# A two-block transformer kernel on one core: six buffers for the u rows in place of four, six places in the weight ring in place of eight

## What is computed

```
def peer(h, w_query, sub_keys, u, v):
    # 8 heads, product keys (2 x 128 sub-keys), top-16 per half -> 256 candidates -> top-16
    ...
        best_s, best_pos = lax.top_k(cand_s, PEER_TOPK)
        expert = jnp.take_along_axis(cand_i, best_pos, axis=-1)
        gate = jax.nn.softmax(best_s, axis=-1)
        u_sel = jnp.take(u, expert, axis=0)
        v_sel = jnp.take(v, expert, axis=0)
        act = jax.nn.gelu(jnp.einsum('btd,bthkd->bthk', hx, u_sel, ...))
        return jnp.einsum('bthk,bthkd->btd', (gate * act).astype(h.dtype), v_sel)
```

## Time and profile before

| | |
|---|---|
| time, median of 3 runs (lowest to highest) | 2198.12 us (2190.49 to 2200.41) |
| span of the profiled execution | 2300.7 us |
| mean granted TensorE clock in it | 0.924 |
| busy: TensorE / weight loads / VectorE / ScalarE / GpSimd | 1853.9 / 1098.1 / 1383.9 / 710.3 / 1045.5 us |
| moved by DMA | 708.03 MB, of it 553.72 MB by the gathers (queue q0) and 150.65 MB by SP's queue (q1) |

### The profile page before, as it was taken

How to read it: one execution, slowest core, us unless ns; L and a number is a source line. 1 busy time by engine, 2 the same in 40 slices (tenths; PEclk the granted TensorE clock), 3 DMA queues, 4 the chain that set the end, 5 groups by cost and what they waited for, 6 DMA issues and landing times. The chain is left out here.

```text
span 2300.7 us, 22295 instructions
## 1 busy us (share of the span) xinstructions
PE 1853.9 (81%) x7068; PEld 1098.1 (48%) x7075; DVE 1383.9 (60%) x3053; ACT 710.3 (31%) x1634; POOL 1045.5 (45%) x1067
## 2 busy tenths in 40 slices
PE   8798766767977787687878866988676898888998
PEld 6554222212643462245445522533232696667996
DVE  2566767645367547755775586555455446456874
ACT  2233433321154113313331233011001344444653
POOL 0365666675447556754666566666666000000000
PEclk7899999997988899988889998999999899998999
DMA  5799999998999999999889999999999354344563
GB/s 185 256 386 376 351 366 350 346 358 308 409 335 352 380 409 368 347 365 387 292 317 402 409 354 350 371 406 381 372 367 370 120 174 123 115 137 133 188 179 116
DMA packets 194851, 708.03 MB, mean 308 GB/s; under 512 B 21784, under 2 KB 23072, under 8 KB 194480
## 3 DMA queue, kind: packets, MB, share of 16 engines
q0 software_dynamic: 152064, 553.72, 63.7%
q1 hardware_dynamic: 40960, 150.65, 19.0%
q10 hardware_dynamic: 1712, 2.24, 0.3%
HBM read 704.81 MB, written 1.06 MB: 307 GB/s over the span
## 5 line engine op out<-in xcount | busy, mean ns | idle before, releaser
L577 PE MATMUL ps<-a,diag 128*128 128x512 f32 (+1 forms) x1872 | 952.9, 647 | 283.7 <-DMA a<-in_peer_v,eidx 114.0
L1738 DVE SCALAR_TENSOR_TENSOR a<-a,ps 128x1024 f32<-128x1024 f32 x512 | 621.4, 1215 | 287.2 <-DMA a<-in_peer_u,eidx 227.4
L406 POOL DMA_INDIRECT a<-in_peer_u,eidx x528 | 527.0, 998 | 494.7 <-DVE a L1738 257.2
L577 PEld LDWEIGHTS ps<-a,diag 128*128 128x128 f32 (+1 forms) x1872 | 351.6, 201 | 825.8 <-issue 678.4
L416 POOL DMA_INDIRECT a<-in_peer_v,eidx x528 | 517.1, 979 | 244.3 <-issue 143.5
L850 PE MATMUL ps<-a_r 128*128 128x256 f32 (+1 forms) x1648 | 392.8, 330 | 19.9 <-DVE a_r L1917 7.3
L1131 ACT ACTIVATE gel<-dots 128x1 f32<-128x1 f32 x528 | 102.6, 201 | 836.9 <-DVE a L1738 482.1
L850 PEld LDWEIGHTS ps<-a_r 128*128 128x128 f32 x1648 | 279.1, 191 | 52.2 <-DVE a_r L1917 8.1
L1911 DVE TENSOR_TENSOR ring_r<-wring,a_r 128x1024 fp32r<-128x1024 f32 x142 | 173.3, 1222 | 138.7 <-ACT a_r L1369 138.6
L1369 ACT ACTIVATE a_r<-wring 128x1024 fp32r<-128x1024 f32 x142 | 149.5, 1054 | 81.8 <-PE ps L850 81.7
L850 PE MATMUL ps<-a_r,ring_r 128*128 128x256 f32 x512 | 144.7, 283 | 0.0
(11 more groups left out here) (263 smaller groups left out, 1583.9 us busy)
## 6 DMA issues: line engine op xcount, KB each, us to landing
wring<-in_units SPq DMA_DIRECT2D x268, 512.0 KB
a<-in_peer_u,eidx POOLq DMA_INDIRECT x528
a<-in_peer_v,eidx POOLq DMA_INDIRECT x528
cs2c<-in_cs SPq DMA_DIRECT2D x1, 1792.0 KB
a<-in_poolm SPq DMA_DIRECT2D x1, 1632.0 KB, 8.9
h<-in_xin SPq DMA_DIRECT2D x2, 512.0 KB, 4.2
bcF<-in_bc_rows SPq DMA_DIRECT2D x2, 512.0 KB, 13.4
cs2c<-in_units SPq DMA_DIRECT2D x2, 512.0 KB, 14.5
```

The costliest lines, as they stand in the source:

```text
L406: g.indirect_dma_start(ug[:, n % NU, :], None, peer_u, bass.IndirectOffsetOnAxis(ap=eidx[:, t, k:k + 1], axis=0))\
L577: last = nc.tensor.matmul(ps[0:P, 6 + j, :], diag[:, pe_slots[n] % 4, 0:P], vg[:, k % NV, j * 512:(j + 1) * 512], start=False, stop=False)
L1738: v.scalar_tensor_tensor(ug[:, n % NU, :], ug[:, n % NU, :], 1.0, hnm if t == 2 else ps2(4), ALU.mult, ALU.mult, accum_out=dots[:, k % 8:k ...
```

## The change

```
-R = 8
-NU = 4
+R = 6
+NU = 6
 NV = 8
...
-                if n == SPLIT0:
+                if n == U0["mem_k"]:
 
                     sp.wait_ge(S("eidx"), tk_number(1, 1))
                     sp.dma_start(memx[:, :, :], mem.rearrange("(t p) d -> p t d", p=128)).then_inc(S("ld_mem"), 16)
                     sp.dma_start(bcL, bc_rows[4:5, :].to_broadcast([128, D])).then_inc(S("ld_g"), 16)
```

## The result

| | median of 4 runs | lowest to highest |
|---|---|---|
| before | 2197.6 us | 2190.49 to 2200.41 |
| after | 2167.69 us | 2166.09 to 2169.31 |

The ratio is 0.9863, 95% interval 0.9848 to 0.9877: 30 us or 1.4% faster. The forecast was 2146, 52 us less than before. Direction and range held, but only 30 of the 52 us came.

The account below looks back on a forecast made before the run. No engine is busy throughout; gathers stall on too few u buffers, leaving DMA under its 409 GB/s ceiling. Parts of 54 + 0 + 0 us off a 2300.7 us span scale 2198.12 to 2146 us, forecast 2110 to 2172, range 2105 to 2187.

Parts of the forecast that it names:

- Part 1: Gather part: two more u buffers shorten GpSimd's waits for dots; 54 us won, between 20 and 88.
- 64 us over 25 stalls: Gather part, stall by stall: smallest of GpSimd's wait, VectorE's wait after it and 5.1 us; five reach the cap.
- The ceiling that the prediction took: Gather stages: the most that deeper buffers can give, summed by stage to 88 us.
- its own example: GpSimd stall at 340.04 to 345.89 us, 4.91 us idle while VectorE is in the top-k; six buffers would remove it.
- the smaller of room and u waits: Each gather stage: gain is the smaller of DMA room below 409 GB/s and VectorE's u waits, or GpSimd's dot waits if less.
- rival (a): VectorE's chain doesn't shorten, as waits saved at dots return at the next piece; 6 us won, 2192 us; chance 0.10.
- the 10 us taken off for the v ring and the shared leads: Gather part: 5 us for more v-row waits on TensorE's sums, 5 us for stalls in a row sharing one lead.
- Part 2: Weight ring of six: cover 8.5 us in the second block, 13 us in the bursts; cost 0, range 0 to 70.
- Rival (d): Weight bursts near 600, 830, 1030, 1270 us: ring of six starves TensorE, 62 us lost, 2231 us; chance 0.06.
- Part 3: Memory rows ahead of their weights from 1409.77 us: six units land by 1433 to 1437, before use at 1451.54; 0 us.
- (b): Gathers have a lower ceiling than 409 GB/s, 370 taken; 21 us won, 2178 us; chance 0.06.
- (c): VectorE's waits for TensorE's late v rows go too; 100 us won, 2102 us; chance 0.08.

Follow-up runs that it names:

- parts 2 and 3 alone: Weight ring cut from eight to six and memory rows loaded ahead of their weights, four u buffers kept, against the kernel before: 2199.06 us, ratio 1.0003.
- the second trace: The kernel before, unchanged, profiled again without the waits on "remote": 2195.97 us timed, ratio 1.0, profiled at 2199.1 us.
- The second group's chip: Chip of four follow-up runs, with the kernel before run beside them; there the kernel before takes 2302.18 us.
- the first trace: Profile of the unchanged kernel before that the prediction read: 2300.7 us where timed runs took 2198, with 339.7 us of waits on "remote".
- u7_r6: Seven u buffers, weight ring of six, memory rows ahead, rotation scratch in the accumulator, against the kernel before: 2269.28 us beside 2302.18, ratio 0.9855.

## Why the prediction was right, and where it was too large

**What bounds it.** Right, and more strictly than the prediction had it. Gathers are issued until 1642 us in after, DMA stands at 392 GB/s of 409 from 60 to 1560 us. Of VectorE's 340 us of u waits that are left only 42 lie in the two low stretches (23.4 in 450 to 700, 18.9 in 1000 to 1240); the others are mostly waits for a full DMA.

**Part 1, the mechanism.** Right: u waits down by 51 us (50 to 60 forecast), the mean GB/s up by 10, the last gather 39 us earlier (50 forecast; it is issued at 1681.26 before and 1642.58 after), the second block untouched. With parts 2 and 3 alone nothing moved.

**Part 1, the size.** This is the step that failed: 54 us in a span of 2300.7, against 30 x 2300.7/2198 = 31. The 64 us over 25 stalls from which it starts stand in no row, so only the sum by stages can be laid beside the traces. The ceiling that the prediction took, beside the room that the second trace and that of after show filled, length x the rise of GB/s/409:

| stage | ceiling taken | filled |
|---|---|---|
| 60 to 100 | not in the sum | 5 |
| 100 to 250 | 9.5 | 0 |
| 250 to 450 | 6.2 | 3 |
| 450 to 700 | 14.7 | -2 |
| 700 to 1000 (650 to 1000 in the prediction) | 18.9 | 9 |
| 1000 to 1240 | 13.2 | 8 |
| 1240 to 1640 (1550 in the traces) | 18.0 | 11 |
| 1640 to 1790 | 7.5 | 0 |
| sum | 88 | 34 |

Two things are in it. The first is that room was read from an execution unlike the timed ones. At 100 to 250 us it showed 383 GB/s and at 1640 on 367 to 372; the second trace of the same kernel has 408 and 409 to 410 there, so in the timed runs these 17 us were never to be had. The table of times gave the warning, 2300.7 beside 2198.12, and the prediction scaled the sum with it instead of asking which idle time belonged to the difference. The per-stall reading stood on the same ground, as its own example shows.

But this doesn't explain the size of the miss. The second group's chip runs like the first trace: 2302 us for the kernel before, and the same waits on "remote" in every trace. There seven u buffers gain 33 us (2302.18 to 2269.28; 24 to 43 by the interval of the ratio), where the prediction has 54 for six. Their trace (`u7_r6`) shows the room still open: 389 GB/s at 100 to 250 us and 366 at 530 to 650, where the first trace has 383 and 359, that is 2 us filled in each of the two against 9.5 and 14.7 taken. So the rule itself failed, the smaller of room and u waits as what is won, also where the room was real.

The second thing is what goes wrong with that rule, and it is seen at 450 to 700 and 1000 to 1240 us. There the second trace of before has both room and u waits, and the smaller of the two was still not what was won. In 450 to 700 VectorE's u waits fell from 46.0 to 23.4 us, and GB/s didn't rise at all. VectorE in order of time in after, at 515 to 545 us:

```profile
517.78 0.35 DVE L1765 TENSOR_SCALAR diag<-cstc,gel,a 128x128 f32<-128x128 f32 x1 [2.63 <-PE ps L577]
...
523.23 0.35 DVE L1765 TENSOR_SCALAR diag<-cstc,gel,a 128x128 f32<-128x128 f32 x1 [3.97 <-PE ps L577]
...
532.42 0.35 DVE L1765 TENSOR_SCALAR diag<-cstc,gel,a 128x128 f32<-128x128 f32 x1 [5.18 <-PE ps L577]
```

and GpSimd beside it:

```profile
517.94 0.99 POOL L416 DMA_INDIRECT a<-in_peer_v,eidx  x1 [3.96 <-PE ps L577]
...
523.39 0.99 POOL L416 DMA_INDIRECT a<-in_peer_v,eidx  x1 [3.21 <-PE ps L577]
...
532.58 0.99 POOL L416 DMA_INDIRECT a<-in_peer_v,eidx  x1 [4.42 <-PE ps L577]
```

TensorE is busy in 29.76 of these 30 us, for example with sixteen matmuls that stand between two of its sums:

```profile
522.96 7.44 PE L480 MATMUL ps<-wring,xT 128*128 128x512 f32 x16
```

```profile
515.00:545.00 30.00, 29.76 (x74) 10.04 (x73) 10.11 (x21) 2.80 (x8) 12.73 (x14) 1.00 0.91 326
```

In the kernel before (second trace) TensorE is busy throughout the same stretch too, but VectorE comes to it later and DMA is still filling the rings, at 411 GB/s:

```profile
515.00:545.00 30.00, 30.00 (x67) 9.31 (x66) 15.23 (x30) 1.42 (x7) 15.09 (x16) 1.00 1.03 411
```

In after VectorE is busy 10 of 30 us and no dot among them waits for a u row; TensorE has other matmuls between its sums, and both VectorE and the v gathers stop at those sums. The lead of 12.9 us at dot 160 is down to 8.7 at dot 176. Seven buffers (322 GB/s in the same 30 us) don't help either. This is rival (a), true for a stage where the prediction weighed it for the whole kernel. What ends the other low stretch, 1000 to 1240 us, is less clear: there u waits fell from 39.2 to 18.9 us, and those on TensorE between the dots (`L1894` 17.4, `L1856` 6.9 us) are what is left.

Whether the 10 us taken off for the v ring and the shared leads were too few can't be told apart from this. The sums' share was put at 5 us; GpSimd's waits on them rose by 31, of which no run shows how much lies on the path. The run with six v places shows that two places of that ring are worth 14.

**Wrong: GpSimd's waits on dots.** They were to fall under 120 us and fell from 297 to 226. That number says little about the time. A queue whose DMA is full makes GpSimd wait somewhere, and each experiment only moves it: 226 and 75 us with six buffers, 145 and 136 with seven, 47 and 224 with eight, and the times lie within 4 us.

**Part 2.** Right at 0: ratio 1.0003, no wait on `wring`. Rival (d) falls. In the burst at 541 to 589 us of after a unit is asked for each 3 us, DMA stands at 408 GB/s from 545 to 600, and a unit lands 7.3 us after its issue (median of 16), where the prediction put 8 to 10 and needed less than 13. With eight places it was 7.4 (median of 20, at 525 to 595 us of the second trace), so that six places shorten the landing isn't seen. Even five places cost at most 3 us and four 22 us, where (d) had 62 for six.

**Part 3.** Right at 0. Behind the memory rows the six units that fit still land before the first use. The DMA issues at 1290 to 1345 us (count, KB each, median us to landing; the seventh unit is asked for after that use) and TensorE's first use of `mem_k`:

```profile
wring<-in_units SPq DMA_DIRECT2D x7, 512.0 KB, 17.2
a<-in_mem SPq DMA_DIRECT2D x1, 1024.0 KB, 10.4
```

```profile
L495 PE MATMUL ps<-xT,wring x64: 379/379/380, 1336.6 to 1365.6; 128*128 128x256 f32 x64
```

Issued from 1295.5 us on, the first unit lands some 13 us later and the sixth some 28 us after the start of the memory rows (23 forecast; both counted from the queue's packets), against a first use at 1336.6.

**Rivals (b) and (c).** (b) falls: with almost nothing but gathers to move, DMA stands at 410 GB/s in after:

```profile
DMA packets 5619, 20.48 MB, mean 410 GB/s; under 512 B 622, under 2 KB 622, under 8 KB 5617
...
q0 software_dynamic: 5617, 20.46, 102.8%
```

(820 to 870 us of after.) The Trainium skill (DMA: Bandwidth & Descriptors, section Bandwidth) has the HBM side bind at about 358 GB/s for a core, and says beside it that a core whose neighbour is idle gets more, 425 GB/s for 16 MB. The 410 over 50 us here agrees with the second sentence; the prediction used the first, as rival (b). Its time of 2178 is nearer to 2168 than the forecast is, but not for its reason. (c) falls with the runs of seven and eight buffers.

**The chances.** 2168 lies in the range and in the forecast's own span of 2110 to 2172, at its edge. What should have been wider is the low side of the gain: that a wait saved at a dot comes back at the next piece was given 0.10 as the whole truth, and nothing as a part of it in every stage.

## What to carry over

Look first whether the profiled execution has the time of the timed runs, and which idle time it has that no cause is recorded for; room and waits that are read from there may not exist in the timed runs (17 of 88 us here). Then ask of each stage what the engine will wait for once this wait is gone: on the chip that runs like the first trace the forecast was as far off (54 for 33) as on the others. With several rings behind one gather queue, what a deeper one can bring is the room that DMA still has in each stage, and only in the stages where that ring, not the next consumer's, ends the wait; the releaser in the stage with the lowest GB/s tells which. Places of a weight ring can be given away as long as a lead over a transfer's landing of 4.2 us is left: with six places the lead in the second block is 8.5 us and the cost 0, with five 5.7 and at most 3, with four 2.8 and 22. The first extra buffer brings most: 20 us, then 11, then 2, the last within the noise.

## What the runs showed of the hardware

The same kernel took 2198 us on two chips and 2302 on a third, each within 1.2% over 9 to 23 runs. In the third chip's traces, as in the first trace of this case, engines stand idle for up to 14.1 us at a time with no releaser but "remote" (GpSimd alone 50.5 us in 21 waits before v gathers with seven u buffers), and the granted clock is 0.905 to 0.924 in place of 0.95. All of the difference lies where gathers run: of the 101.6 us between the two traces of the kernel before, 101.6 lie before the end of the last dot (1789.1 and 1687.5 us), and the second block takes 511.6 us in both. What it is wasn't found, nor is it on record which chip gave the first trace. The gain of deeper buffers was the same in ratio on both kinds (seven buffers, 0.9855 and 0.9849), which speaks against a gain that comes from covering those stalls.
